# Three of four output pairs of the down projection by seven products, in groups 1 and 2 of each layer

## The reference

```
hdn = jnp.square(jax.nn.relu(x @ w_up))              # 1024 -> 4096
x = layer_norm(DEEPNORM_ALPHA * x + hdn @ w_down)    # 4096 -> 1024
```

## Time and profile before

| what | value |
|---|---|
| median of three runs | 2130.46 us (2130.21 to 2131.23) |
| the profiled execution | 2129.4 us |
| its span, first to last instruction | 2127.6 us |
| granted TensorE clock, mean | 0.998 |
| matmuls | 15716 |
| PE busy | 2106.3 us (99%) |
| POOL, DVE, ACT busy | 62%, 49%, 25% |

### The profile page before, as it was taken

One profiled execution on the slowest core, in us unless ns is written; L12 is line 12 of the kernel. 1 busy time (PEld: TensorE's weight loads), 2 busy tenths in 40 slices (PEclk: granted clock), 3 DMA queues, 4 the chain that ended last, 5 costly groups with the idle time before them and its releaser, 6 DMA issues.

```text
span 2127.6 us, 38066 instructions
## 1 busy us (share of the span) xinstructions
PE 2106.3 (99%) x15716; PEld 2044.7 (96%) x15716; DVE 1047.9 (49%) x1669; ACT 524.9 (25%) x935; POOL 1311.1 (62%) x1549
## 2 busy tenths in 40 slices
PE   8999999999999999999999999999999999999997
PEld 8898999999999999999998989999999999999997
DVE  6156300534278873626781571006424787726257
ACT  5121121041014141414241210210410231514133
POOL 6744558645683947466757346676456748475574
PEclk9999999999999999999999999999999999999999
DMA  5415324234231323222223153332342213222331
GB/s 178 132 52 168 127 82 139 76 107 161 95 100 60 100 80 100 80 84 80 96 72 119 59 173 110 115 120 76 113 169 84 96 60 99 80 81 79 100 100 45
DMA packets 200324, 215.41 MB, mean 101 GB/s; under 512 B 5600, under 2 KB 192992, under 8 KB 200160
## 3 DMA queue, kind: packets, MB, share of 16 engines
q1 hardware_dynamic: 170688, 172.84, 25.2%
q10 hardware_dynamic: 29472, 40.20, 5.5%
HBM read 199.06 MB, written 13.97 MB: 100 GB/s over the span
## 4 chain that ended last, share of the span: by engine, by line
PE 96%; DVE 3%; ACT 0%; ACTq 0%; issue 0%; POOL 0%; DVEq 0%
PE gp L583 53%; PE gp L1108 13%; PE gp L606 9%; PE gp L597 7%; PE qb L686 7%; PE gp L760 3%; PE qb L760 2%; PE gp L950 1%; PE gp L938 1%; PE qb L726 1%; DVE r L2158 1%; DVE x_lo L2064 0%; DVE r L2058 0%; DVE r L2055 0%; DVE m_lo L1666 0%; DVE m_hi L1665 0%
## 5 line engine op out<-in xcount | busy, mean ns | idle before, releaser
L466 POOL TENSOR_TENSOR w_lo<-stage,w_hi 128x256 fp32r<-128x256 f32 x1008 | 815.9, 840 | 90.7 <-ACT w_hi L1202 70.7
L463 POOL TENSOR_SCALAR w_hi<-stage 128x1024 fp32r<-128x1024 f32 x240 | 253.1, 1054 | 497.8 <-PE gp L583 244.5
L583 PE MATMUL gp<-b_hi,w_hi 128*128 128x288 f32 x1408 | 321.6, 295 | 0.0
L583 PE MATMUL gp<-x_hi,w_hi 128*128 128x288 f32 x1408 | 321.3, 295 | 0.0
L583 PE MATMUL gp<-b_hi,w_lo 128*128 128x288 f32 x1408 | 318.5, 293 | 0.0
L583 PE MATMUL gp<-b_lo,w_hi 128*128 128x288 f32 x1408 | 318.5, 293 | 0.0
L583 PE MATMUL gp<-x_hi,w_lo 128*128 128x288 f32 x1408 | 318.4, 293 | 0.0
L583 PE MATMUL gp<-x_lo,w_hi 128*128 128x288 f32 x1408 | 318.4, 293 | 0.0
L583 PEld LDWEIGHTS gp<-b_hi,w_hi 128*128 128x128 f32 x1408 | 231.6, 188 | 2.4 <-issue 2.2
L583 PEld LDWEIGHTS gp<-x_hi,w_hi 128*128 128x128 f32 x1408 | 231.4, 188 | 2.3 <-issue 2.1
L583 PEld LDWEIGHTS gp<-b_lo,w_hi 128*128 128x128 f32 x1408 | 231.5, 188 | 1.0 <-issue 1.0
(11 more groups left out here) (299 smaller groups left out, 4272.3 us busy)
## 6 DMA issues: line engine op xcount, KB each, us to landing
stage<-in_w_in SPq DMA_DIRECT2D x54, 1024.0 KB, 5.4
stage<-in_w_up SPq DMA_DIRECT2D x32, 1024.0 KB, 5.3
stage<-in_w_down SPq DMA_DIRECT2D x32, 1024.0 KB, 5.0
stage<-in_w_in SPq DMA_DIRECT2D x40, 256.0 KB, 4.3
stage<-in_w_ret_out SPq DMA_DIRECT2D x8, 1024.0 KB, 5.3
stage<-in_w_mem_kv SPq DMA_DIRECT2D x8, 1024.0 KB, 5.2
stage<-in_w_out SPq DMA_DIRECT2D x8, 1024.0 KB, 5.0
s_in_c<-in_ret_state ACTq DMA_DIRECT2D x8, 512.0 KB, 4.8
```

The lines of the kernel that those rows point to most:

```text
L463: nc.gpsimd.tensor_scalar(hi, raw, 1.0, 1.0, ALU.mult, ALU.mult).then_inc(hi_done, 1)
L466: ins = nc.gpsimd.tensor_tensor(lo[:, k:k + 2, :], raw[:, k:k + 2, :], hi[:, k:k + 2, :].bitcast(F32), ALU.subtract)
L583: last = mm(gp[:, 2 * (i % 2) + half, 0:HALF], w[:, i % 4, k * P:(k + 1) * P], x(k, half), start=(k == n == 0), stop=(k == nk - 1 and n == 2))
```

## The change

In groups 1 and 2 of both layers output tiles 0 and 1 of the down projection stay plain (now both with the halves by turns), and tiles 2 to 7 become three pairs by seven products, down pairs 1 to 3. The blocks are tiles 2k and 2k+1 of the hidden features, so that each up pair p gives one of the four k. For each of them the four sums of its blocks have to be made and split: POOL makes three (`hidden_sums`), DVE one (`hidden_sum`), ACT the high part (`hidden_sums_high`), DVE the low part (`hidden_sums_low`). Those of up pairs 0 and 1 are made while the up projection still runs, those of pairs 2 and 3 behind it. The raw sums of pairs 0 to 2 go through `s_raw`, those of pair 3 through `part`. Room for the results comes from the table of constants, from `tmp`, and from parts of x that are no longer read; so the table is loaded once more before layer 1 needs it. DVE adds eight quarter results of a down pair to `r` (`quarter_added`), ACT copies two of them to `part` first (`keep_down`), and the first pair of the next group's up projection is prepared behind down pair 3.

```diff
+        def hidden_sums(l, g, p):
+            t, to, no = relu_of(p), raw_sums(p), hidden_no(l, g, p)
+            (a11, a12), (a21, a22) = ([t[:, i, COLS[h]] for i in range(2)] for h in range(2))
+            pool.wait_ge(act_made, 2 * up_no(l, g, p) + 2)
...
+            if p == 3:
+                pool.wait_ge(quarter_made, 4 * up_no(l, g, p) + 4)
+            elif no:
+                pool.wait_ge(h_split, no)
+            minus = nc.gpsimd.tensor_tensor
+            minus(to[:, 0, :], a21, a22, ALU.add).then_inc(h_pool, 1)
+            pool.wait_ge(h_pool, 3 * no + 1)
+            minus(to[:, 1, :], to[:, 0, :], a11, ALU.subtract).then_inc(h_pool, 1)
+            pool.wait_ge(h_pool, 3 * no + 2)
+            minus(to[:, 3, :], a12, to[:, 1, :], ALU.subtract).then_inc(h_pool, 1)
...
                     raw_low(l, g, p, 2)
...
+                    pair_split(l, g, p, False)
+                    if p >= 2 and g < 3:
+                        hidden_sums(l, g, p - 2)
...
-                split_four(l, T_FF + 16 * g + 8, behind=(g, pair_no(l, g, 3)))
-                split_four(l, T_FF + 16 * g + 12)
...
+                split_four(l, T_FF + 16 * g + 8, behind=(g, pair_no(l, g, 3)), slots=2)
+                hidden_sums(l, g, 2)
+                hidden_sums(l, g, 3)
+                for p in range(1, 4):
+                    for i in range(3):
+                        raw_low(l, g, p, i, True)
+                    pair_split(l, g, p, True)
...
+                if down and p == 1:
+                    pe.wait_ge(h_split, hidden_no(l, g, 3) + 1)
...
-                pe.wait_ge(part_in, 4 * q + 1)
+                kept(1, down_added, 8 * d + 1)
                 one(3, a, rows_sum(1), False)
...
+                seven = g in (1, 2)
-                for i in range(4 if last else 8):
+                for i in range(4 if last else 2 if seven else 8):
...
-                                                         + 2)) if i == 0 else None, by_half=(g > 0 and i == 1),
...
+                                                         + 2)) if i == 0 else None, by_half=(last and i == 1),
...
+                if seven:
+                    for p in range(1, 4):
+                        seven_products(g, p, True)
...
+            def hidden_sums_high(g, p):
+                no = hidden_no(l, g, p)
+                act.wait_ge(h_pool, 3 * no + 3)
+                act.wait_ge(h_dve, no + 1)
+                act_fn(high_sums(p), raw_sums(p)[:, :, :], ACT.Copy).then_inc(h_high, 1)
...
+                if g == 3 and l < DEPTH - 1:
+                    act.wait_ge(prod_done, 7 * pair_no(l, 2, 3, True) + 7)
+                    act.dma_start(table_sb[:, K_COS:K_DMP], table[:, K_COS:K_DMP]).then_inc(rope_in, 16)
+                    act.dma_start(table_sb[:, K_DMP:K_ALL], table[:, K_DMP:K_ALL]).then_inc(table_in, 16)
...
                         seven_high(g, p + 1, 1)
+                    if p >= 2 and g < 3:
+                        hidden_sums_high(g, p - 2)
...
+                raw_to_bank(g, 1, True)
+                hidden_sums_high(g, 2)
+                seven_high(g, 1, 0, True)
+                seven_high(g, 1, 1, True)
+                hidden_sums_high(g, 3)
+                for n in range(2, 7):
+                    seven_high(g, 1, n, True)
...
+            def hidden_sum(g, p):      
...
+                vec_.tensor_tensor(raw_sums(p)[:, 2, :], t[:, 0, COLS[0]], t[:, 0, COLS[1]], ALU.subtract).then_inc(h_dve, 1)
+
+            def hidden_sums_low(g, p):
+                no = hidden_no(l, g, p)
+                dve.wait_ge(h_high, no + 1)
+                for first, lo in low_sums(p):
+                    many = slice(first, first + lo.shape[1])
+                    ins = vec_.tensor_tensor(lo, raw_sums(p)[:, many, :], high_sums(p)[:, many, :].bitcast(F32), ALU.subtract)
+                ins.then_inc(h_split, 1)
...
+            def down_pair(g, p):
...
+                made(1)
+                quarter_added(g, p, 0)
+                quarter_added(g, p, 1)
+                low(1)
+                made(2)
+                made(3)
+                quarter_added(g, p, 2)
+                low(2)
+                made(4)
+                quarter_added(g, p, 3)
+                quarter_added(g, p, 4)
+                low(3)
+                quarter_added(g, p, 5)
+                quarter_added(g, p, 6)
+                quarter_added(g, p, 7)
+                low(4)
...
                     quarter_out(g, p, 0)
+                    if g < 3 and p >= 2:
+                        hidden_sums_low(g, p - 2)
+                        hidden_sum(g, p - 1)
...
+                    if g < 3 and p == 0:
+                        hidden_sum(g, 0)
...
+                elif g < 3:
+                    hidden_sum(g, 3)
+                    for i in range(1, 5):
+                        weight_sum(g, 1, i, True)
+                    hidden_sums_low(g, 2)
+                    down(g, 0)
+                    hidden_sums_low(g, 3)
+                    down(g, 1)
+                    for i in range(1, 5):
+                        sum_low(g, 1, i, True)
+                    for p in range(1, 4):
+                        down_pair(g, p)
```

More of the change, by code:

```diff
@@ L342, in value_bank, with quarter, pair_landed, seven_free @@
         return (gp[:, 3, :], qb[:, 2, :], qb[:, 3, :], qb[:, 1, :], gp[:, 2, :])[t]
[L344 to L348, removed]
+    def quarter(p, k_half, column, down=False):
+        rows = slice(k_half, KT, 2) if down else slice(4 * k_half, 4 * k_half + 4)
+        return stage[:, p % 2, rows, column * P:(column + 1) * P]
+    def pair_landed(eng, l, g, p, down=False):
+        t = first_tile(g, p, down)
         eng.wait_ge(stage_full[p % 2], l * (TILES * 4) + (t - t % 4) * 4 + 16)
-    def seven_free(eng, l, g, p, n):
-        if p == 0:
-            tile_is_done(eng, l, T_FF + 16 * g - 4 + n // 2)
+    def seven_free(eng, l, g, p, n, down=False):
+        if (down and p == 1 and n < 4) or (not down and p == 0 and g == 1):
+            tile_is_done(eng, l, first_tile(g, p, down) - (2 if down else 4) + n // 2)
         else:
-            eng.wait_ge(prod_done, 7 * pair_no(l, g, p - 1) + n + 1)
+            eng.wait_ge(prod_done, 7 * (pair_no(l, g, p, down) - 1) + n + 1)
     def t_sum(i):
@@ L444, in _, with split_four @@
         pool.sem_inc(split_done, RING)
-        def split_four(l, first, rows=(KT, KT), high_made=False, behind=None):
+        def split_four(l, first, rows=(KT, KT), high_made=False, behind=None, slots=RING):
             n = l * TILES + first
-            for s in range(RING):
+            for s in range(slots):
                 if behind is None:
@@ L489, in split_rows, with raw_low @@
                 pool.sem_inc(stage_full[half], 16)
-        def raw_low(l, g, p, i):
+        def raw_low(l, g, p, i, down=False):
             n = (0, 1, 4)[i]
-            q = pair_no(l, g, p)
-            raw = quarter(p, *SEVEN[n])
+            q = pair_no(l, g, p, down)
+            raw = quarter(p, *SEVEN[n], down)
             hi, lo = seven_slot(w_hi, n), seven_slot(w_lo, n)
@@ L572, in turns, with product @@
             return [(k, n, half) for k in ks for n in range(3) for half in range(2)]
[L574 removed]
+        def product(l, t, half_t, i, hi, lo, nk=KT, wait_k=None, within=None, by_half=False, banks=None):
             pe.wait_ge(split_done, l * TILES + t + 1 + RING)
@@ L1117, in seven_products @@
                 one(1, b, rows_of(1, 0), True)
-                if g == 1 and p == 0:
+                if g == 1 and p == 0 and not down:
                     pe.wait_ge(s_split, l * 4 + 4)
+                if down and p == 1:
+                    pe.wait_ge(h_split, hidden_no(l, g, 3) + 1)
                 pe.wait_ge(t_split, 4 * q + 1)
@@ L1606, in keep_part, with keep_down @@
                 if q:
                     act.wait_ge(quarter_made, 4 * (q - 1) + 4)
+                if g > 1 and p == 0:
+                    act.wait_ge(down_added, 8 * down_no(l, g - 1, 3) + 8)
                 act_fn(part[:, i, :], gp[:, bank, 0:HALF], ACT.Copy).then_inc(part_in, 1)
+            def keep_down(g, p, n, bank, i):
+                d = down_no(l, g, p)
+                act.wait_ge(prod_done, 7 * pair_no(l, g, p, True) + n + 1)
+                act.wait_ge(h_split, hidden_no(l, g, 3) + 1)
+                if p > 1:
+                    act.wait_ge(down_added, 8 * (d - 1) + 8)
+                act_fn(part[:, i, :], gp[:, bank, 0:HALF], ACT.Copy).then_inc(down_part, 1)
@@ L2169, in down @@
                 tile_is_done(dve, l, g * 16 + T_FF + 8 + m)
-                vec_.tensor_tensor(halves(r[:, m, :]), halves(r[:, m, :]), pair(m % 2),
-                                   ALU.add).then_inc(pair_free[m % 2], 1)
+                if g == 2:
+                    for half, bank in enumerate(PLAIN_TWO[m]):
+                        ins = vec_.tensor_tensor(r[:, m, COLS[half]], r[:, m, COLS[half]], gp[:, bank, 0:HALF], ALU.add)
+                else:
```

(2 more changed lines are left out.)

233 lines of the change are left out of this document (165 added, 68 removed).

## The result

The changed kernel takes 2140.09 us (median of four executions, 2139.89 to 2141.42) against 2130.34 us (four, 2129.14 to 2131.23) for the kernel before: ratio 1.0047, 95% interval 1.0035 to 1.006, so it is 9.8 us slower. The forecast was 2134.4 us, inside 2122 to 2144, with slower as the likeliest of the three outcomes; the increase came out at more than twice the 4.0 us that were summed up, and the time just above the 2130 to 2139 us that the forecast gave itself.

What follows compares the result with a forecast made beforehand. TensorE, busy 99% of the span, was taken as the bound. Per group, 5.2 us of waits against 4.2 us saved made four groups 4.0 us longer: 2133.4 us profiled, 2134.4 us as median, range 2122 to 2144.

Steps and rivals of the forecast that it cites:

- three outcomes: Whole kernel against no change: slower above 2134.7 us, chance 0.46; the same, 0.36; faster below 2126.2 us, 0.18.
- Saved matmuls: Down projection: 45.98 instead of 50.19 us a group, 4.21 us less, 16.8 us over four groups if PE never waits.
- Turns: DVE instructions with two SBUF inputs alternate with POOL's; one of each together advance by some 1.22 us.
- the turns hardly bite: Faster rival: new work falls into DVE's and POOL's idle stretches, waits under 3.1 us a group; about 2118 us, chance 0.17.
- the longer turn: Slower rival: each turn lasts the whole recorded duration, about 0.74 + 0.75 us, waits 7.4 us a group; 2143 us, chance 0.20.
- First place: Up pairs 2 and 3: PE waits 0.2 us at pair 2, 0.85 and 1.05 us at pair 3; sum 2.1 us.
- each square waits 0.3 us: Up pair 1: two of POOL's sums of pair 0 meet DVE's squares, each delayed 0.3 us.
- the slack of 0.27 us: Up pairs 1 and 2: last quarter ends 0.27 us before the next pair's product 1; going negative, it costs 0.2 us.
- Second place: Plain tiles into the first down pair: waits of 0.4, 1.1, 1.0 and 0.6 us; sum 3.1 us a group.
- At nothing: Down pairs 2 and 3, their loads, the table reload and ACT's additions: no PE waits; bank-freeing quarters end 0.9 us early.
- The sum: Per group 5.2 us of waits against 4.2 us saved: 1.0 us longer, 4.0 us for four groups.

Runs made afterwards that it cites:

- psum_low: Changed kernel with the low parts of the sums of up pairs 0 and 1 reading PSUM instead of the raw sums in SBUF; 2133.68 us, ratio 1.0016.
- no_pool_sums: Changed kernel with POOL's three sums a set left out, POOL only raising their semaphore; 2126.84 us, ratio 0.9984 to the kernel before.
- rebuilt_bank: Changed kernel reordered, raw sums given separate room, two plain tiles' high parts moved to ACT, bank-freeing quarter added first; 2120.89 us, ratio 0.9956 to the kernel before.
- bank_first: Changed kernel with DVE adding product 4's bank-freeing quarter ahead of the last weight sum and kept quarter in a down pair; 2135.94 us, ratio 1.0028.
- one half of the reordering: Changed kernel with either half alone: separate raw-sum room and later low parts, 2135.04 us; or ACT's high parts, earlier pair-2 sums and first result, 2135.16 us.

## Why the prediction was right in kind and short in size

**Saved matmuls.** 96.73 less 6.0 us of waits is 90.7 us, 4.1 us less than before; forecast 4.21. Right.

**Turns.** The term that made it slower was right. Two subtractions of 128x576 beside POOL took 2.50 us again, the first low part 1.81 us on average where 1.8 was laid out, and `psum_low` took the turn away and got the 0.4 and 0.7 us back. The rival "the turns hardly bite" is out by that. The 2143 us of "the longer turn" lie nearer to the result than 2134.4, but not by its mechanism: the rounds of 0.74 and 0.75 us took 1.25 us (two in those 2.50, DVE's timeline), not 1.49. That a round is 0.60 us of DVE and 0.62 of POOL, as the prediction splits it, no row shows.

```profile
820.53 2.50 DVE L2467 TENSOR_TENSOR b_lo<-relu_odd,b_hi 128x576 fp32r<-128x576 f32 x2
```

**First place.** Product 0 of up pair 3 came as laid out (0.83 for 0.85). Products 1 were under-sized: 0.58 for 0.2 and 1.28 for 1.05. The step that failed is "each square waits 0.3 us", and with it the 0.16 us laid out from a release until PE runs again. The timelines of DVE and POOL in the changed kernel:

```profile
792.73 1.32 DVE L2436 SCALAR_TENSOR_TENSOR relu_odd<-relu_odd 128x576 f32<-128x576 f32 x1
...
794.57 0.44 DVE L2388 TENSOR_TENSOR relu_odd<-part,gp 128x288 f32<-128x288 f32 x1
795.16 1.05 DVE L2436 SCALAR_TENSOR_TENSOR relu_odd<-relu_odd 128x576 f32<-128x576 f32 x1
```

```profile
792.63 0.80 POOL L560 TENSOR_TENSOR s_raw<-relu 128x288 f32<-128x288 f32 x1 [0.35 <-POOL w_lo L540]
793.51 1.21 POOL L562 TENSOR_TENSOR s_raw<-s_raw,relu 128x288 f32<-128x288 f32 x1
```

A square takes 0.76 us alone. The first one met a sum of 0.80 us that had begun 0.1 us earlier and lost 0.56 us, the second 0.29. The hand-over from DVE's quarter to PE is 0.28 us: 0.20 from the quarter's end (795.01) to PE's start (795.22), and 0.08 by which the next matmul comes late. 0.56 less the slack of 0.27 us that the prediction found, and with that hand-over, makes 0.57 of the 0.58 us; without the sums (`no_pool_sums`) the wait is nil. The square ahead of product 1 of pair 3 took 1.20 us and lost 0.44: 0.14 more than laid out, and 0.12 more for the hand-over, against 0.23 us missed there. In group 2 of layer 0 the first square of pair 1 begins 0.2 us ahead of the sum, not behind it, and keeps its 0.76 us while the sum takes 1.21: no wait there, and 0.99 us at product 0 of pair 3.

The Trainium skill (SBUF — State Buffer, "Who interferes with whom") lets issue order decide who blocks. The trace agrees: in `rebuilt_bank` DVE's low part came first and kept its 1.36 us, and POOL's sum of 0.80 us took 1.89 (timelines of POOL and of DVE).

```profile
807.64 1.89 POOL L567 TENSOR_TENSOR x_two<-relu,x_two 128x288 f32<-128x288 f32 x1
```

```profile
807.51 1.36 DVE L2385 TENSOR_TENSOR h_four<-s_raw,h_four 128x1152 fp32r<-128x1152 f32 x1
```

**Second place.** Forecast 0.4, 1.1, 1.0 and 0.6 us, measured 0.29, 0.95, 0.98 and 0.61. Right, and `no_pool_sums` shows POOL's sums as the cause of the middle two: without them both waits are nil.

**"At nothing".** Wrong for down pair 3 and the next up pair: the quarters were said to end 0.9 us before PE wants the bank; the one that counts ends 0.04 us before, and the hand-over of 0.28 us (855.95 to 856.15, and the next matmul) leaves a gap of 0.24, twice a group. `bank_first` takes both away.

**The sum.** Waits of 6.0 for 5.2 us and 0.1 us less saved make about 1.9 instead of 1.0 us a group, 7.7 instead of 4.0 us. In the profiled pair the rhythm adds 76.80 less 74.88 us for the 576 matmuls from 694 us, 1.9 us, and 0.6 us for the 192 at 1090 us. 7.7 + 2.5 = 10.2 of 10.5 us; 0.3 us was not assigned. So of the 5.7 us between forecast and median 3.7 are mis-sized terms of the sum: the squares, the hand-over, and what stood at nothing. For the other 2.0 us the rhythm is a candidate, which the prediction did not know; only profiled executions show it, so whether it is in the medians stays open. A hint: the medians of all eight versions lie 0.4 to 2.4 us further below the changed kernel's than their four groups in the traces account for. That the outcome "slower" came as forecast is not luck, since nearly all of the waits stand at the places named; that the range held owes something to its upper end, which was drawn for the longer turn.

## What to carry to other kernels

Saved TensorE work is worth what the other engines' queues leave of it: with PE at 99% the new element-wise work, small beside the idle time, gave back more than the 16.8 us saved, and the same work in another order, with two copies moved to ACT, gave 9.6 us net. Lay the queues out in program order, charge turns wherever DVE reads two SBUF operands beside POOL, and follow a stall to the next place before pricing a fix: one half of the reordering mended its place and paid most of it at the next. When a bank is said to be free in time, take the time of the very instruction that raises the semaphore: a slack below the hand-over (0.04 against 0.28 us here) is a gap.

## What the runs showed of the hardware

Long runs of fp32r matmuls of 128x288 start every 130.0 or every 133.3 ns at a granted clock of 1.00, one rhythm for the whole stretch. Over the 576 matmuls of group 0 this is 1.9 us; in twelve traces 7 of 24 such stretches had the slower one, among them layer 0 in one execution of the changed kernel and not in the other, so the program alone does not set it. The 192 at 1090 us had it in 7 of 12 traces, in both of the changed kernel and in neither of the kernel before. The kernel before had the slower rhythm in none of its six stretches, the changed kernel and its versions in 14 of 30; whether that is chance stays open, and so does what sets the rhythm.
